# Projecting the first two tiles from the raw input, with x in column halves, the first weights by tile and the small loads reordered

## What is computed

```python
h = rms_norm(x, g_mix)                     # x * rsqrt(mean(x*x) + eps) * gain
proj = h @ w_in                            # 1024 x 9232 columns: qa ka va za beta a qd kd vd gate_a gate_b
qkv = silu(causal_depthwise_conv(qa|ka|va, conv_w))
oa = gated_delta_rule(...)                 # from qkv, beta, a
od = diff_attention(qd, kd, vd, lam, rel_bias[t5_bucket(rel)])
x = x + (sigmoid(gate_a)*oa + sigmoid(gate_b)*od) @ w_o
x = x + moe_ffn(rms_norm(x, g_ffn), ...)   # top 4 of 32 experts, clamped SwiGLU
```

## Time and profile before

| | |
|---|---|
| median of 3 runs | 1306.62 us (1305.88 to 1310.32) |
| the profiled execution | 1308.24 us |
| its span | 1306.3 us |
| TensorE busy | 96% |
| VectorE, ScalarE, POOL busy | 28%, 22%, 4% |
| DMA, mean | 346 GB/s |
| chain that ended last | TensorE 59%, DMA 33% (w_up loads 26%), VectorE 4% |

### The profile page before, as it was taken

One profiled execution on the slowest core, in us unless ns is written; L12 is line 12 of the kernel. 1 busy time (PEld: TensorE's weight loads), 2 busy tenths in 40 slices (PEclk: granted clock), 3 DMA queues, 4 the chain that ended last, 5 costly groups with the idle time before them and its releaser, 6 DMA issues.

```text
span 1306.3 us, 14461 instructions
## 1 busy us (share of the span) xinstructions
PE 1247.7 (96%) x5617; PEld 545.5 (42%) x5617; DVE 367.7 (28%) x1016; ACT 283.4 (22%) x559; POOL 47.6 (4%) x102
## 2 busy tenths in 40 slices
PE   9999999999999999999999999989999998999997
PEld 7887456644453333333333333333333333333332
DVE  4576825664332112211121111211111111221111
ACT  3231122243122121211221112211111121121112
POOL 3040110110000000000000000000000000000000
PEclk9999999999999999999999999999999999999999
DMA  7772533374748999999999999999999999999996
GB/s 234 138 230 74 200 99 111 104 282 160 303 186 359 428 429 427 428 426 428 427 428 427 428 427 428 427 428 428 426 428 428 428 428 426 427 428 428 428 426 259
DMA packets 57770, 452.58 MB, mean 346 GB/s; under 512 B 10760, under 2 KB 10904, under 8 KB 33136
## 3 DMA queue, kind: packets, MB, share of 16 engines
q1 hardware_dynamic: 53552, 447.24, 82.8%
q0 software_dynamic: 1568, 3.72, 1.7%
q10 hardware_dynamic: 2592, 0.79, 0.3%
HBM read 448.17 MB, written 3.15 MB: 345 GB/s over the span
## 4 chain that ended last, share of the span: by engine, by line
PE 59%; DMA 33%; DVE 4%; ACT 2%; issue 1%; SPq 0%; ACTq 0%; PEldq 0%
DMA ring<-in_w_up_dram 26%; PE pb L1472 19%; PE pb L1509 11%; PE pb L1205 9%; PE pb L1186 4%; DMA last_slot<-in_w_up_dram 4%; PE pb L1435 4%; DMA ring<-in_w_in_dram 3%; PE pb L1423 2%; PE pb L1351 2%; PE pb L1172 2%; DVE ring L910 1%; DVE ring L909 1%; PE pb L1429 1%; PE pb L1494 1%
## 5 line engine op out<-in xcount | busy, mean ns | idle before, releaser
L1472 PE MATMUL pb<-ring,buf_a 128*64 128x512 f32 x1856 | 418.2, 595 | 26.8 <-DMA ring<-in_w_up_dram 26.8
L1472 PEld LDWEIGHTS pb<-ring,buf_a 128*64 128x64 f32 x1856 | 128.4, 136 | 276.2 <-issue 218.2
L1131 DVE TENSOR_SCALAR buf_a<-pb 128x256 f32<-128x256 f32 x64 | 26.9, 421 | 722.9 <-PE pb L1472 722.9
L1509 PE MATMUL pb<-ring,buf_b 128*64 128x512 f32 x944 | 209.7, 595 | 7.7 <-ACT buf_b L756 6.9
L1205 PE MATMUL pb<-ring,last_slot 128*128 128x512 f32 x384 | 173.3, 597 | 0.9 <-PE pb L1205 0.6
L1509 PEld LDWEIGHTS pb<-ring,buf_b 128*64 128x64 f32 x944 | 65.4, 137 | 131.4 <-issue 116.3
L735 ACT ACT_TABLE_LOAD x32 | 41.1, 1283 | 304.9 <-PE pb L1423 304.9
L1205 PEld LDWEIGHTS pb<-ring,last_slot 128*128 128x128 f32 x384 | 69.8, 190 | 78.4 <-issue 77.4
L1186 PE MATMUL pb<-last_slot,ring 128*128 128x256 f32 x384 | 89.7, 388 | 1.1 <-DMA ring<-in_w_in_dram 1.1
L1186 PEld LDWEIGHTS pb<-last_slot,ring 128*128 128x128 f32 x384 | 72.7, 193 | 11.1 <-issue 1.4
L758 ACT COPY buf_b<-pb 128x512 f32<-128x512 f32 x32 | 18.7, 585 | 222.7 <-PE pb L1509 222.7
(11 more groups left out here) (286 smaller groups left out, 875.5 us busy)
## 6 DMA issues: line engine op xcount, KB each, us to landing
ring<-in_w_up_dram SPq DMA_DIRECT2D x116, 2048.0 KB, 43.2
ring<-in_w_down_dram SPq DMA_DIRECT2D x59, 2048.0 KB, 46.7
ring<-in_w_in_dram SPq DMA_DIRECT2D x18, 2048.0 KB, 8.3
last_slot<-in_w_up_dram SPq DMA_DIRECT2D x12, 2048.0 KB, 47.0
last_slot<-in_w_down_dram SPq DMA_DIRECT2D x5, 2048.0 KB, 35.8
ring<-in_w_o_dram SPq DMA_DIRECT2D x2, 2048.0 KB, 14.2
t_rows<-ring POOLq DMA_DIRECT2D x1, 1536.0 KB, 34.8
xt<-in_x_dram SPq DMA_DIRECT2D x2, 512.0 KB, 4.2
```

What stands on the lines that cost most here:

```text
L1131: v.tensor_scalar(glu[:, cols], pairs[:, :, 0], LIMIT, None, ALU.min).then_inc(s_glu, 1)
L1472: ins = mm(pb[64 * hf:64 * hf + 64, n_, :], xg[:, c, :], slot(s)[:, at_:at_ + 512], start=False, stop=(c == KC - 1), skip_group_check=True)
L1509: ins = mm(pb[64 * hf:64 * hf + 64, 2, :], actT[:, j, hf_in, :], slot(s)[:, at_:at_ + 512], start=(c == 0), stop=(c == KC - 1), skip_group ...
```

## The change

- **x** is loaded in two halves of columns (both row blocks in each), and between them the first 128 columns of piece 0 in two halves of rows, then its second 128 columns, `wba`, and the rest of piece 0. g_mix is loaded by ScalarE, ahead of the parameters.
- **Small loads** (rel_bias, dt_bias, a_log, lambdas) are issued by SP behind piece 0 and ahead of pieces 1 and 2, without a wait.
- **Transposes** are of x itself: TensorE turns the first half, then parameters, then within tile 0 the second. VectorE multiplies by the gain and writes `xT`.
- **Tiles 0 and 1** (NRAW = 2) are projected from `xT`. The factor `rr` is turned into rows (`rr_rows`, token along the free axis, the same in all partitions) by two transposes between tiles 0 and 1 and a copy of ScalarE; VectorE multiplies the two tiles by it as it takes them from PSUM into `raw`, in ScalarE's place. Then VectorE multiplies `xT` by `rr_rows` in two halves into `hT`, for tile 2 and all that follow.
- WARM is 8; `ba` comes after tile 3 instead of tile 2.

```diff
-    WARM = 20
+    WARM = 8
+    NRAW = 2
-    extra = {2: [("ba",)], 4: [("gc",)], ...
+    extra = {3: [("ba",)], 4: [("gc",)], ...
@@ SP
-            sp.dma_start(rows2[0:8, :], g_mix[0:1]...).then_inc(s_gmx, 16)
...
-            for b in range(NB):
-                sp.dma_start(xt[:, b, :], x[0, b * P:(b + 1) * P, :]).then_inc(s_x[b], 16)
-            for n in range(NPIECE + 2):
+            for i in range(2):
+                sp.dma_start(xt[:, :, 512 * i:512 * i + 512], x_half(i)).then_inc(s_x[i], 16)
+                sp.dma_start(*first_tile_half(i)).then_inc(s_w0[i], 16)
+            sp.dma_start(piece_at(0)[:, :, P:2 * P], w_piece(0)[:, :, P:2 * P]).then_inc(s_w1, 16)
+            sp.dma_start(wba[:, :, :], win[:, C_BA:C_BA + 2 * H].rearrange("(k p) n -> p k n", p=P)).then_inc(s_wba, 16)
+            sp.dma_start(piece_at(0)[:, :, 2 * P:], w_piece(0)[:, :, 2 * P:]).then_inc(s_piece[0], 16)
+            sp.dma_start(rowbuf[:, 384:384 + NBUCK], rel_bias.rearrange("b h -> h b")).then_inc(s_rbld, 16)
+            sp.dma_start(dtb, dt_bias[0:1, :].to_broadcast([P, H])).then_inc(s_small, 16)
+            sp.dma_start(alog, a_log[0:1, :].to_broadcast([P, H])).then_inc(s_small, 16)
+            for i, src in enumerate((lambda_q1, lambda_k1, lambda_q2, lambda_k2)):
+                sp.dma_start(lamrow[:, i, :], src[0:1, :].to_broadcast([P, 64])).then_inc(s_lamld, 16)
+            for n in range(1, NPIECE + 2):
@@ ScalarE
+            act_e.dma_start(rows2[0:8, :], g_mix[0:1]...).then_inc(s_gmx, 16)
-                sc.activation(xn[:, b, :], xt[:, b, :], ACT.Square, accum_out=ss[:, b:b + 1]).then_inc(s_ss, 1)
+            for i in range(2):
+                act_e.wait_ge(s_x[i], 16)
+                for b in range(NB):
+                    sc.activation(xsq[:, b, 512 * i:512 * i + 512], xt[...], ACT.Square, accum_out=ssx[:, i, b:b + 1]).then_inc(s_ss, 1)
-            act_e.wait_ge(s_piece[0], 16)
-            act_e.dma_start(wba[:, :, :], ...).then_inc(s_wba, 16)
...
+            act_e.wait_ge(s_rrp, 1)
+            sc.copy(rr_rows, pb[:, 7, P:P + T]).then_inc(s_rrr, 1)
@@ VectorE
-            for b in range(NB):
-                v.tensor_scalar(xn[:, b, :], xt[:, b, :], rr[:, b:b + 1], None, ALU.mult).then_inc(s_xn, 1)
+            def take_raw_tile(t):
+                dve.wait_ge(s_pj, t + 1)
+                v.tensor_tensor(raw[:, t, :], pb[:, t, 0:T], rr_rows, ALU.mult).then_inc(s_pjf, 1)
+            dve.wait_ge(s_rrr, 1)
+            dve.wait_ge(s_xT, 4)
+            take_raw_tile(0)
+            for i in range(2):
+                v.tensor_tensor(hT[:, 4 * i:4 * i + 4, :], xT[:, 4 * i:4 * i + 4, :], rr_rows[:, None, :].to_broadcast([P, 4, T]), ALU.mult).then_inc(s_hT, 1)
@@ TensorE
+                    w, rows = piece_at(n), xT if t < NRAW else hT
                     for c in range(KC):
                         if t == 0 and c % 4 == 0:
-                            pe.wait_ge(s_hT, 2 + c // 2)
+                            pe.wait_ge(s_xT, 2 + c // 2)
+                            pe.wait_ge(s_w0[c // 4], 16)
+                        elif t == 0 and c == 2:
+                            x_turn(1)
+                        elif t == 1 and c == 0:
+                            rr_rows_turn()
+                        elif t == NRAW and c % 4 == 0:
+                            pe.wait_ge(s_hT, 1 + c // 4)
```

More of the change, by code:

```diff
@@ L204, in block_kernel @@
         junk = ring[:, 3, 2 * D:3 * D]
-        xn = buf_a[:, :].rearrange("p (b d) -> p b d", b=NB)
-        qdt = xn
-        OD = xn
+        xsq = buf_a[:, :].rearrange("p (b d) -> p b d", b=NB)
+        qdt = xsq
+        OD = xsq
+        xT = ring[:, 2, 2 * D:].rearrange("p (c t) -> p c t", c=KC)
+        rr_rows = ring[:, 1, 0:T]
         kdt = buf_b[:, :].rearrange("p (b d) -> p b d", b=NB)
@@ L245, in block_kernel @@
         gffn_pairs = small(8)
+        ssx = small(4).rearrange("p (i b) -> p i b", i=2)
         ssp = small(4).rearrange("p (b n) -> p b n", b=2)
@@ L275, in block_kernel @@
         idx_u = idx8.bitcast(U32)
-        s_x = [sem(f"x_loaded_{b}") for b in range(NB)]
+        s_x = [sem(f"x_half_loaded_{i}") for i in range(2)]
         s_par, s_small, s_lamld, s_rbld, s_wba = sem("params_loaded"), sem("small_loaded"), sem("lambdas_loaded"), sem("rel_bias_loaded"), sem("wba_loaded")
@@ L286, in block_kernel @@
         s_t5st, s_t5 = sem("t5_rows_stored"), sem("t5_bias_loaded")
-        s_ss, s_xn, s_tr, s_hT = sem("row_squares"), sem("rows_normalised"), sem("transposes_done"), sem("hT_blocks_ready")
+        s_ss, s_tr, s_xT, s_hT = sem("row_squares"), sem("transposes_done"), sem("scaled_xT_blocks_ready"), sem("hT_halves_ready")
+        s_w0, s_w1 = [sem(f"first_tile_half_loaded_{i}") for i in range(2)], sem("second_tile_loaded")
+        s_rrk, s_rrp, s_rrr = sem("rr_ready"), sem("rr_rows_turned"), sem("rr_rows_ready")
         s_ptr, s_parc = sem("params_transposed"), sem("params_ready")
@@ L369, in load @@
                 sp.dma_start(slot(s), slab(s)).then_inc(s_slab[s % NSLOT], 16)
-            sp.dma_start(rows2[0:8, :], g_mix[0:1].rearrange("a (t p) -> (a t) p", p=P)).then_inc(s_gmx, 16)
             def front_dead(i):
@@ L545, in link @@
                 act_e.wait_ge(s_act, n[0])
+            act_e.dma_start(rows2[0:8, :], g_mix[0:1].rearrange("a (t p) -> (a t) p", p=P)).then_inc(s_gmx, 16)
             act_e.dma_start(par_rows[0:96, :], conv_w[0].rearrange("w (t p) -> (w t) p", p=P)).then_inc(s_par, 16)
@@ L603, in _ @@
                     t = it[1]
-                    act_e.wait_ge(s_pj, t + 1)
-                    if t >= 3:
-                        act_e.wait_ge(s_conv, t - 2)
-                    sc.copy(raw[:, t % 3, :], pb[:, t % 2, 0:T]).then_inc(s_pjf, 1)
+                    if t >= NRAW:
+                        act_e.wait_ge(s_pj, t + 1)
+                        act_e.wait_ge(s_pjf, t)
+                        if t >= 3:
+                            act_e.wait_ge(s_conv, t - 2)
+                        sc.copy(raw[:, t % 3, :], pb[:, t % 2, 0:T]).then_inc(s_pjf, 1)
                     if t >= 1:
@@ L783, in roots @@
                 link(v.tensor_tensor(y, y, w, ALU.mult))
-            dve.wait_ge(s_ss, NB)
-            link(v.tensor_scalar(ss, ss, 1.0 / D, EPS, ALU.mult, ALU.add))
-            roots("x", rr, ss, rt2)
-            for b in range(NB):
-                v.tensor_scalar(xn[:, b, :], xt[:, b, :], rr[:, b:b + 1], None, ALU.mult).then_inc(s_xn, 1)
             dve.wait_ge(s_gmt, 1)
@@ L1153, in _, with x_turn, rr_rows_turn @@
             nc.tensor.transpose(pb[:, 7, 0:8], rows2[0:8, :], ident[0:8, 0:8]).then_inc(s_gmt, 1)
[L1154 to L1163 removed]
+            def x_turn(i):
+                pe.wait_ge(s_x[i], 16)
+                for b in range(NB):
+                    for c in range(4):
+                        ins = nc.tensor.transpose(pb[:, 2 + 2 * i + b, c * P:(c + 1) * P], xt[:, b, (4 * i + c) * P:(4 * i + c + 1) * P], ident)
+                    ins.then_inc(s_tr, 1)
+            x_turn(0)
+            pe.wait_ge(s_par, 16 * 6)
+            nc.tensor.transpose(pb[:, 6, 0:96], par_rows[0:96, :], ident[0:96, 0:96])
+            nc.tensor.transpose(pb[:, 6, 128:146], rows2[0:18, :], ident[0:18, 0:18]).then_inc(s_ptr, 1)
+            def rr_rows_turn():
+                pe.wait_ge(s_rrk, 1)
+                for b in range(NB):
+                    ins = nc.tensor.transpose(pb[:, 7, P + b * P:2 * P + b * P], rr[:, b:b + 1].to_broadcast([P, P]), ident)
+                ins.then_inc(s_rrp, 1)
             def startA(it):
```

43 lines of the change are left out of this document (20 added, 23 removed).

## The result

The changed kernel takes **1320.3 us** (median of 4 executions, 1319.34 to 1321.11), against 1306.81 us for the kernel before on the same chip (1305.88 to 1310.32). The ratio is 1.0094 with a 95% interval of 1.0075 to 1.0112: slower by 13.5 us, 0.9%.

A forecast was written before the change was run, and what follows sets the result against it. The expert weight stream, started by the front and without slack, was taken to set the end. +5.7 - 1.1 + 1.7 + 0.5 = +6.8 us on 1306.62 gave 1313.4 us; range 1301 to 1317, the forecast's own 1310.5 to 1317.

The forecast's parts named there:

- The head, 3.5 us: Work up to tile 7: tile 0 starts at 7.4, the head gains about 3.5 us, tile 8 could start at 47.3.
- t_rows issued at 18.2, first packets at 20.3: POOL's store of the bias rows: issued 12 us sooner, at 18.2 instead of 30.44, and starting at 20.3.
- rival 3: SP's queue: small loads not early, rel_bias at 18 or later, t_rows misses piece 2; 1304 us, chance 0.08 with others.
- Pieces 1 and 2 from 14.9: w_in loads on SP's queue: pieces 1 and 2 run from 14.9, 1.9 us after piece 0 lands.
- Piece 2 at 56.5, +5.7: w_in load before tile 8: sharing engines with t_rows, it lands at 56.5; tile 8 starts then instead of 50.76, +5.7 us.
- Rival 1: DMA queues: the later t_rows lets piece 2 pass, tile 8 starts at 47.3; -4.6 us, 1302.0 us, chance 0.22.
- Piece 3's wait gone, -1.1: w_in load before tile 12: it lands at about 62, before tile 12 wants it, so 1.1 us of waiting go.
- The clock, +1.7 (bounds 0 and 3.4): TensorE at tile 8: after standing still for 9 us its clock falls to 0.50, costing 1.7 us.
- POOL's split beside VectorE, +0.5 (bounds 0 and 2): Tile 8's convolution on VectorE: POOL's split of b_up comes 10 us sooner, lies beside it and costs 0.5 us.
- The end moves with tile 12: Expert weight stream behind the front: it has no gap to absorb anything, so a front d longer moves the end by d.
- Rival 2: t_rows against piece 2: 2 to 3 us of slip lands piece 2 at 47 to 54; 1306 us, chance 0.15.

The follow-up runs named there:

- the repeat: The changed kernel run once more without an edit: median 1319.55 us, ratio 1.0084 to the kernel before.
- the split held: The changed kernel, with POOL's split of b_up waiting until the decay matrix's exponentials are done: 1317.51 us, ratio 1.0072 to the kernel before.
- the wide store with the split held: The changed kernel with t_rows stored by sixteen engines and POOL's split of b_up after the decay matrix's second exponential: 1306.5 us, ratio 0.9992 to the kernel before.

## Why the prediction was wrong

The sign was right, and so was the mechanism up to tile 8: the bias rows released the store early, and the store held up piece 2. What follows tile 8 was mis-sized. The sum was 6 to 7 us too small, and the result lies above the range. Step by step:

- **The head, 3.5 us.** Forecast: tile 0 at 7.4, tile 4 at 27.4, tile 8 ready at 47.3. Measured: 8.15, 29.57, 49.2, so 1.6 us gained. In the repeat: 7.78, 27.62, 47.6, close to the forecast. Between the two lies the clock: TensorE waited 1.25 and 1.17 us for the parameters, until 7.75 and 7.38 instead of 7.2; in 9.70:11.40 of the first execution it then stood at 0.50, in the repeat at 1.00, and tile 0's first products and the transposes in it took 1.70 + 1.91 us against 1.13 + 1.04. The low clock fell on tile 4 as forecast (5.12). SP's issuing was too cheap, costed at half a us each; with short rows in the queue it took up to 3.18. No wait of TensorE before tile 8 comes from it, but piece 0 landed at 14.3 instead of 13.0:

```profile
3.54 1.77 SPq L403 DMA_DIRECT2D wba<-in_w_in_dram  x1
5.36 3.18 SPq L404 DMA_DIRECT2D ring<-in_w_in_dram  x1
8.58 1.70 SPq L405 DMA_DIRECT2D ring<-in_rel_bias_dram  x1
```

  As piece 2 set tile 8's start, none of it counted in the end.
- **t_rows issued at 18.2, first packets at 20.3.** Measured: 22.89, and 27 to 28. rel_bias came 1.1 us later than forecast (14.64), POOL's 32 copies took 7.70 instead of 4.08 us (I had taken without asking what VectorE did beside it), and the first packets came 4 to 5 us after the issue instead of 2. The issue after 22 was the prediction's own sign for rival 3, and the pieces in the same queue were late with it; the store did not miss piece 2 all the same.
- **Pieces 1 and 2 from 14.9.** They flow from 19 to 20, since the small loads hold SP's queue. This slip of 5 us cancels most of the store's 7. Had only the store slipped, piece 2 would have been through (an estimate: the 128 rows for each engine of pieces 1 and 2, at 0.085 us each from 14.9, are done at 25.8). That the collision came out as forecast is thus in part luck.
- **Piece 2 at 56.5, +5.7.** Measured: 55.12 and 57.73, +4.4 and +7.0: right, and with the measured starts the same reckoning gives about the same. In 19:27 q1 moved 2.85 MB, 3.0 by 27.5; the 1.2 MB left of 4.2 are 37 packets for each engine, at 0.79 us with a packet of the store each: 27.5 + 29 = 56.7. In the kernel with the small loads back some 0.6 MB are left at 30.8, 20 packets for each engine: 46.6, before tile 8 wants it. The turns of 9 to 17 descriptors that the prediction quotes from the Trainium skill do not show here either: each packet of q1 is one row of 2 KB, and there are 42 of them beside 44 of q0. Rival 1, which had their time, fell with them.
- **Piece 3's wait gone, -1.1.** Right.
- **The clock, +1.7 (bounds 0 and 3.4).** Sized for one fall at tile 8; tile 8 alone cost 2.3. The second fall, +3.0 at tile 11, was not in the sum at all. The pause of 5.2 us before the sums comes ahead of it, 3.6 us longer than before because VectorE is late; with the split held it is 1.56 again and tile 11 takes 3.70. How much of this fall belongs to the clash stays open, as the wide store with the split held has tile 11 at 5.39 behind the same 1.56.
- **POOL's split beside VectorE, +0.5 (bounds 0 and 2).** This is **the step that failed**. It cost 3.7 us, and with the fall of the clock behind the longer pause 6.7. In the repeat, where tile 8 came later and missed part of the split, the same two terms are 1.5 and 1.7 us, and the wait for piece 2 is the larger part with 7.0 of 11.3. So the size of this step varies with the execution, but both times it is several times the 0.5 of the sum. The row was in hand: the earlier trace rows has 3.41 us against 1.52 for three steps, an excess of 1.9 for one part of a convolution, and that should have been the middle, not the upper bound. Instead I treated a clash of two engines at the side as small, since the split is "POOL's". The prediction even says that only a late tile 4 could make it slower than forecast. The clash wasn't at the side: tile 8's convolution, decay matrix, exponentials and tile 9's copy are one chain, and TensorE stands at its end.
- **The end moves with tile 12.** +12.07 at the experts' first product and +12.14 at their last: right for this loss, apart from 0.8 us that the last transfer added. For gains of 2 us at tile 12 the profiles agree (last block 2.2 to 2.6 us sooner), the medians do not show them.

With the measured sizes the forecast's own sum gives 4.4 - 1.1 + 2.3 + 3.7 + 3.0 = 12.3 and 1306.6 + 12.3 + 0.8 = 1319.7.

The rivals: that the later queue waits (rival 1) fell, by q0's and q1's packets in 42:46. Rival 2 (half of it) had the store's slip, and the slip was larger than it asked for, but it had not seen that the pieces would slip with the store. Rival 3 saw that the pieces stand in the same queue as the small loads, and took the store to miss piece 2 all the same.

## What to carry to other kernels

A load that is moved earlier starts everything that waits for it earlier, and what was harmless late may be in the way early: here 1 KB of bias released a store of 1536 KB that holds eight DMA engines for 35 us, in front of a transfer that had 15 us to spare. Look at each store's outermost dimension and spread it over sixteen partitions, or hold the store with a wait on the transfer that matters more; here either took the whole loss away, and neither made the kernel faster than before. And when a delay has been found, follow it through the chain that it starts: the wait itself was 4.4 us of 12 in one execution and 7.0 of 11 in the other, the rest were a clash and two falls of the clock behind it.
